# Openings of the matmul sections behind a layer norm: when chunk 0 is multiplied and when x is transposed

## The reference

```python
x = layer_norm(ALPHA * x + mixed @ w_out, ln1_g, ln1_b)
h = square(relu(x @ w_up))                       # third block; gated in the second, absent in the first
x = layer_norm(ALPHA * x + h @ w_down, ln2_g, ln2_b)
```

## Time and profile before

| what | value |
|---|---|
| median of 3 runs | 3687.05 us (3685.27 to 3688.78) |
| profiled execution, its own time | 3686.9 us |
| its span | 3684.8 us |
| mean granted TensorE clock | 0.976 |
| TensorE matmul busy | 3476.2 us, 94% |
| VectorE, ScalarE busy | 2239.9 us (61%), 1580.1 us (43%) |
| HBM read | 604.29 MB, 165 GB/s over the span |

### The profile page before, as it was taken

How to read it: one execution, slowest core, us unless ns; L and a number is a source line. 1 busy time by engine, 2 the same in 40 slices (tenths; PEclk the granted TensorE clock), 3 DMA queues, 4 the chain that set the end, 5 groups by cost and what they waited for, 6 DMA issues and landing times.

```text
span 3684.8 us, 56355 instructions
## 1 busy us (share of the span) xinstructions
PE 3476.2 (94%) x22856; PEld 3189.9 (87%) x22856; DVE 2239.9 (61%) x2908; ACT 1580.1 (43%) x1876; POOL 6.3 (0%) x9
## 2 busy tenths in 40 slices
PE   8999999999999856789999999989999999999998
PEld 8898998888798846679999988889999799998886
DVE  6667555555659966655444456776766644446766
ACT  4345544344333341233333345543445344445554
POOL 0000000000000000000000000000000000000000
PEclk9999999999999988999999999999999999999999
DMA  6455566666665520055666656654545566655554
GB/s 195 125 163 152 160 195 195 207 200 191 194 178 148 155 71 0 23 177 183 182 182 182 182 170 193 192 156 132 166 144 177 176 203 182 182 182 177 191 195 150
DMA packets 324281, 608.69 MB, mean 165 GB/s; under 512 B 28365, under 2 KB 42703, under 8 KB 322840
## 3 DMA queue, kind: packets, MB, share of 16 engines
q1 hardware_dynamic: 317752, 587.46, 52.9%
q10 hardware_dynamic: 6368, 19.01, 1.3%
HBM read 604.29 MB, written 2.10 MB: 165 GB/s over the span
## 4 chain that ended last, share of the span: by engine, by line
PE 85%; DVE 9%; issue 3%; ACT 2%; DMA 1%; DVEq 0%; SPq 0%; ACTq 0%
PE ps L569 26%; PE ps L570 26%; PE ps L571 26%; DVE arena L1543 2%; DVE w_lo L1537 1%; DVE xtok L1543 1%; DVE arena L1537 1%; ACT w_hi L1126 1%; PE ps L1041 1%; DVE arena L2298 1%; PE ps L1052 1%; PE ps L1049 1%; DMA ring<-in_w_in 1%; PE ps L741 0%; PE ps L872 0%
## 5 line engine op out<-in xcount | busy, mean ns | idle before, releaser
L1537 DVE TENSOR_TENSOR w_lo<-ring,w_hi 128x1024 fp32r<-128x1024 f32 (+2 forms) x1144 | 1371.0, 1202 | 1262.2 <-ACT w_hi L1126 1074.8
L1126 ACT ACTIVATE w_hi<-ring 128x1024 fp32r<-128x1024 f32 (+2 forms) x1144 | 1187.8, 1042 | 1704.9 <-PE ps L569 1636.8
L569 PE MATMUL ps<-x_hi,w_hi 128*128 128x256 f32 x4816 | 1380.1, 287 | 22.4 <-DVE w_lo L1537 21.0
L570 PE MATMUL ps<-x_lo,w_hi 128*128 128x256 f32 x4816 | 1370.6, 285 | 0.0
L571 PE MATMUL ps<-x_hi,w_lo 128*128 128x256 f32 x4816 | 1370.1, 284 | 0.0
L569 PEld LDWEIGHTS ps<-x_hi,w_hi 128*128 128x128 f32 x4816 | 931.4, 193 | 29.6 <-DVE w_lo L1537 20.3
L570 PEld LDWEIGHTS ps<-x_lo,w_hi 128*128 128x128 f32 x4816 | 931.5, 193 | 0.9 <-issue 0.2
L571 PEld LDWEIGHTS ps<-x_hi,w_lo 128*128 128x128 f32 x4816 | 930.8, 193 | 0.3
L569 PE MATMUL ps<-w_hi,h_hi 128*128 128x512 f32 x864 | 337.9, 391 | 9.5 <-DVE h_lo L1537 9.5
L570 PE MATMUL ps<-w_lo,h_hi 128*128 128x512 f32 x864 | 337.6, 391 | 0.0
L571 PE MATMUL ps<-w_hi,h_lo 128*128 128x512 f32 x864 | 337.4, 390 | 0.0
(11 more groups left out here) (330 smaller groups left out, 2598.8 us busy)
## 6 DMA issues: line engine op xcount, KB each, us to landing
ring<-in_w_in SPq DMA_DIRECT2D x416, 512.0 KB, 3.7
ring<-in_w_down SPq DMA_DIRECT2D x216, 512.0 KB, 4.2
ring<-in_w_gate_up SPq DMA_DIRECT2D x176, 512.0 KB, 3.7
ring<-in_w_up SPq DMA_DIRECT2D x128, 512.0 KB, 3.8
ring<-in_w_out SPq DMA_DIRECT2D x64, 512.0 KB, 4.5
ring<-in_w_branch SPq DMA_DIRECT2D x36, 512.0 KB, 4.3
ring<-in_w_in SPq DMA_DIRECT2D x48, 384.0 KB, 3.2
ring<-in_w_o SPq DMA_DIRECT2D x32, 512.0 KB, 4.7
```

Source lines behind the costliest of these rows:

```text
L569: first = pe.matmul(out, left[0], right[0], start=start, stop=False)
L570: pe.matmul(out, left[0], right[1], start=False, stop=False)
L1126: last = act.activation(w_hi[:, s, :, 0:width], ring[:, s, :, 0:width], ACT.Copy)
L1537: return dve.tensor_tensor(o, a, b, op)
```

## The change

Chunk 0 of an opening is multiplied once groups 0 and 1 are transposed. Groups 2 and 3 are transposed before chunk 1, groups 4 and 5 before chunk 3, groups 6 and 7 before chunk 5. ScalarE copies groups 0 and 1 before w_hi of chunk 3, 2 and 3 before chunk 4, 4 and 5 before chunk 6, 6 and 7 before chunk 8, and calls `then` behind these. VectorE has the order: groups 0 and 1, quarter 1, w_lo of chunk 3; groups 2 and 3, quarter 2, w_lo of chunk 4; quarter 3, w_lo of chunk 5; groups 4 and 5, w_lo of chunk 6; w_lo of chunk 7; groups 6 and 7, w_lo of chunk 8. The norm itself ends with quarter 0, and the last one is followed by quarters 1 to 3. The same orders hold at the start, where there is no norm.

```diff
--- before.py
+++ after.py
@@ -580,8 +580,8 @@
                     s = (g + c) % RING
                     if opens is not None:
                         normed, base = opens
-                        if c in (2, 4):
-                            transpose_x(range(c + 2, c + 4), normed)
+                        if c in (1, 3, 5):
+                            transpose_x(range(c + 1, c + 3), normed)
                         pe.wait_ge(xTp_used, base + c + 1)
                     chunk(g + c, more)
                     x = src(c, s)
@@ -619,7 +619,7 @@
             def project_opening(name, normed=True, side=None):
 
                 sec, base = plan[name], n.now(xTp_used)
-                transpose_x(range(4), normed)
+                transpose_x(range(2), normed)
                 for t, u, it in tiles_of(pe, sec, side is not None, opens=True):
                     first = isinstance(t, int) and t == 0
                     pe.wait_ge(tile_free[u], sec.tiles[u] + it)
@@ -1150,10 +1150,12 @@
             def opening(t, then=None):
 
                 def before(c):
-                    if c < 3:
-                        take_x(range(4, 4) if c == 0 and t is None else range(4) if c == 0 else range(2 * c + 2, 2 * c + 4))
-                    elif c == 3 and then is not None:
-                        then()
+                    if c in (0, 1) and t is not None:
+                        take_x(range(2 * c, 2 * c + 2))
+                    elif c in (3, 5):
+                        take_x(range(c + 1, c + 3))
+                        if c == 5 and then is not None:
+                            then()
                 return before if t is None or isinstance(t, int) and t == 0 else None
 
             def prime_hidden(name):
@@ -1622,14 +1624,13 @@
             def opening(t):
 
                 def before(c):
-                    if c == 0:
-                        take_x(range(2))
-                        normed_cols(2)
-                        take_x(range(2, 4))
-                    elif c < 3:
-                        if c == 1:
-                            normed_cols(3)
-                        take_x(range(2 * c + 2, 2 * c + 4))
+                    if c in (0, 1):
+                        take_x(range(2 * c, 2 * c + 2))
+                        normed_cols(c + 1)
+                    elif c == 2:
+                        normed_cols(3)
+                    elif c in (3, 5):
+                        take_x(range(c + 1, c + 3))
                 return before if isinstance(t, int) and t == 0 else None
 
             def prime_hidden(name, times):
@@ -1828,7 +1829,6 @@
                 dve.reciprocal(stat[:, 28:30], stat[:, 28:30]).then_inc(rstd_ready, 1)
                 dve.wait_ge(rstd_ready, n.next(rstd_ready))
                 scaled(0)
-                normed_cols(1)
 
             def third_mixers():
 
@@ -2113,9 +2113,9 @@
             def at_start(t):
 
                 def before(c):
-                    if t == 0 and c in (1, 2):
-                        take_x(range(2 * c + 2, 2 * c + 4))
-                    elif t == 1 or c > 2:
+                    if t == 0 and c in (3, 5):
+                        take_x(range(c + 1, c + 3))
+                    elif t == 1 or c > 5:
                         next(made, None)
                 return before
 
@@ -2390,8 +2390,8 @@
                 splits(plan["up3"], u, it, before=opening(t))
             prime_hidden("down3", 1)
             layer_norm("down3", hidden=True)
-            normed_cols(2)
-            normed_cols(3)
+            for c in range(1, 4):
+                normed_cols(c)
 
 
 # ---- launch: one core; inputs and outputs as the reference has them ----
```

## The result

| | before | after |
|---|---|---|
| median | 3687.72 us (18 runs) | 3695.85 us (18 runs) |
| ratio | | 1.0022, 95% interval 1.0015 to 1.0028 |
| span of the profiled execution | 3684.8 us | 3694.4 us |

The change costs 8.1 us, 0.22%. The forecast was 3686.4 us within 3681.5 to 3690.5, and no difference that can be told; the time lies outside the range.

A forecast was written before the change was run, and what follows sets the result against it. TensorE, busy 94% of the span, was taken as the bound. Clock cases summed to +0.9 (-3.5 + 4.4) or -2.3 us (-6.7 + 4.4); the middle, given as -0.5, took 3686.9 to 3686.4 us, range 3681.5 to 3690.5.

The forecast's parts named there:

- Part 5: The start (aqk): chunk 0 begins at about 8.8 instead of 10.68, waited off later; taken as 0, possible cost 3.3 us.
- Part 3: VectorE's order behind the norms: a new wait for x_lo before chunk 4, +0.85 us in each opening.
- Part 1: Behind each norm: chunk 0 starts 2.15 us behind the first transposes instead of 3.82, 1.67 us earlier in four openings.
- (a): Openings behind norms: the clock rises when it did, so the earlier start wins 3.5 us; the sum is +0.9 us.
- Part 2: TensorE's transposes between chunks behind norms: three sets instead of two, one more uncovered, +0.64 us an opening.
- Part 4: ScalarE's queue and the ring loads on SP behind norms: nothing lost, with about 1 us of cover in qkm.
- rival 4: Openings: chunk 0 still stands for something else, such as w_lo; only +1.11 x 4 remains: 3691.3 us, chance 0.05.
- rival 3: SP's queue at the start: late w_lo of chunk 2 makes chunk 8 start 3.3 us later: 3689.7 us, chance 0.15.
- 1, the clock following the matmuls: Openings behind norms: the clock rises as much earlier as the matmuls, winning 6.7 us: 3684.6 us, chance 0.2.
- 2: Openings behind norms: no new stall before chunk 4, 0.85 us less in each: 3683.0 us, chance 0.1.

The follow-up runs named there:

- all ahead: The change with, at the start, groups 4 and 5 taken before chunk 5's split, 6 and 7 before chunk 7's, 13 constants steps kept: 3689.66 us, ratio 1.0005.
- parameters later: The change with the small parameter loads at the start issued by SP behind the second tile's ring loads instead of the first's: 3692.01 us, ratio 1.0015.
- behind the norms: The change with the start in its old order and, behind norms, groups 4 and 5 taken ahead of chunk 5's split: 3686.98 us, ratio 0.9994.
- start alone: The kernel before, with the change's new order at the start only: 3695.26 us, ratio 1.0018.
- groups 4 and 5 ahead: The change with groups 4 and 5 at the start taken on ScalarE and VectorE ahead of chunk 5's split: 3697.48 us, ratio 1.0027.

## Why the prediction was wrong, and where it was right

**Part 5, the start, failed.** It took nothing and named one danger, the block in SP's queue, priced at 3.3 us. Its own steps held: w_lo of chunk 2 done at 17.6, and the block ends when it did. Two terms were missing.

- *What the moved copies stand behind.* The part followed TensorE and SP past the moved steps, but not ScalarE and VectorE. At the start the w_hi of chunk 5 waits for a load (24.45), and the copies of groups 4 and 5 had been ahead of it in the kernel before. The missing term is a wait of 3.0 us and the half clock after it; "all ahead" and "parameters later" each remove it, one by the order of the copies and one by the loads. At the 14th w_hi copy 2.7 us of it are left, since chunk 0 began earlier and the 0.97 us before chunk 8 are saved. Part 3 had the right form of this sum for the openings behind norms, where weights are there in time.
- *The constants.* The diff moves `next(made)` from `c > 2` to `c > 5`, and no part priced it: 1.8 us of wait, and 1.6 of half clock behind it (6.1 - 2.7 = 3.4 between the 14th and the 20th copy). Keeping the steps gave back 2.8 us by the medians, each taken against the kernel before beside it.

The rest of the 7.7 us, 1.6, is a half-clock stretch behind a wait of 1.84 us at 132.7, which the kernel before has too without losing the clock. Why it loses the clock in one and not in the other stays open.

**Part 1 was right**: chunk 0 at 2.21 us for 2.15. Of its two cases (a) came: on average the rise did not move with the matmuls (below).

**Part 2 was right**, three sets of 0.64.

**Part 3 was right in form and a little high**: the wait before chunk 4 is 0.69 to 0.71 us, forecast 0.85, and "behind the norms" shows that it is VectorE's order. Behind wo VectorE's side of that sum, from the transposes behind chunk 0 to chunk 4, measured 10.90 us (1020.46 to 1031.36) for 10.87; TensorE's own side was 10.21 for 10.02. Chunk 5 starts 21.89, 21.42, 22.04 and 22.18 us behind the first transposes in the changed kernel. Over the six kernels timed with the change's order behind the norms it is 21.84 on average, over the three with the old order 21.47: the change costs 0.37 us in an opening, 1.5 us in all, where the forecast had -0.5 with 0.9 for case (a). It is not the same in each: 0.13, 0.31, 0.23 and 0.79, and in the last one (up3) the clock rose 1.15 us later on average, for no reason that the runs show. So the 1.5 us is not well known.

**Part 4 was right**: nothing moved on ScalarE's queue behind the norms is seen to hold TensorE; the wait for kif_lo in qkm is 1.19 us, 1.30 before.

Two sums of the prediction do not come out as written. The middle of +0.9 and -2.3 is -0.7, not -0.5. And the upper end of the range does not follow from its cases: leaving out a tenth of the chance (rival 4 and a part of rival 3) leaves 3689.7, leaving out a tenth of the width leaves 3690.3, and with the 1.8 added these give 3691.5 or 3692.1, not 3690.5. Neither would have brought 3695.85 inside.

**The rivals.** 1, the clock following the matmuls, fell: in those six kernels and the three with groups 4 and 5 ahead, 36 openings, matmuls begin 1.62 us earlier (2.21 for 3.83) and the clock rises 6.97 us behind the first transposes on average, against 7.06 in 12 openings of the old order. The four openings of one execution are not independent, but the means of the nine executions run from 6.4 to 7.5 us and those of the three from 7.0 to 7.1, and a rise 1.62 us earlier would be at 5.4. By the rule of the Trainium skill ("TensorE: Matmul & The Clock Gate", Part 4: PE-mode transpose), that a transpose does not count as activity for the clock as a matmul does, the rise would have come those 1.6 us earlier; measured is 0.09, so these traces do not bear it out. 2 fell, as the wait is there. 3 was at the right place, on the right side, with the wrong queue. 4 fell.

## What to carry to other kernels

When a copy is moved later in an in-order engine's list, write down every instruction that it now stands behind, on each engine that takes part, and ask for each what it waits for itself: a copy of what TensorE needs next was put behind a weight that was still on its way. A hand-written order also carries passengers (here the constants in the same `elif`); count them before and after. The opening at the start is not the same case as one behind a norm: there the weights are still being loaded while the orders run.

## What was not expected of the hardware

- Which of these short waits is followed by half clock is not told by its length. The wait of 2.81 us at line 950 was followed by half clock in the change, in "start alone" and in "groups 4 and 5 ahead", but not in "parameters later", where it is as long. Waits of 1.8 to 1.9 us in the attention steps (between 99 and 133 us) were followed by half clock, worth about 1.6 us, in 8 of the 12 profiled kernels and not in the kernel before.
- The clock came back 5.05 to 8.26 us behind the first transposes in the openings of the kernels tried, a spread of 3.2 us that follows none of the edits. It makes single profiles of an opening differ by up to half of that (a microsecond at half clock is worth half of one), more than the effects sought here; only averages over openings can tell, and small ones remain uncertain.
- Where it ends, a block of SP's queue did not move when its start did: 16.25 to 26.19 before, 19.30 to 26.07 after. In "parameters later", where all of the small loads are issued later, it stands from 26.98 to 34.46. This fits a wait for the small loads issued ahead of it, but no run separates them.
